# Where an S5 mixer hands over to a gated unit: weight loads, tap shifts and first products in another order

## What is computed

```
def s5_mixer(u, lam_re, lam_im, log_dt, b_re, b_im, c_re, c_im, d_skip, w_glu):
    ...
    bu = jnp.einsum('blgh,gph->blgp', ug, b_bar)
    _, states = lax.associative_scan(_ssm_combine, (a_seq, bu), axis=1)
    y = jnp.einsum('blgp,ghp->blgh', states, c).real.reshape(bsz, length, D_MODEL)
    y = y + d_skip.astype(f32) * u.astype(f32)
    y = jax.nn.gelu(y).astype(u.dtype)
    val, gate = jnp.split(y @ w_glu, 2, axis=-1)
    return val * jax.nn.sigmoid(gate)
...
    for i in range(DEPTH):
        h = rmsnorm(x, norm_mix[i])
        ...
        x = x + mix.astype(x.dtype)
        x = x + swiglu(rmsnorm(x, norm_ffn[i]), ffn_w_gate_up[i], ffn_w_down[i]).astype(x.dtype)
```

## Time and profile before

| | |
|---|---|
| Median of 3 runs | 1955.73 us (1953.88 to 1959.09) |
| Profiled execution, span | 1956.0 us |
| PE busy | 1897.2 us (97%) |
| DVE, ACT, POOL busy | 773.4, 809.7, 849.5 us (40 to 43%) |
| mean granted PE clock | 0.988 of full speed |
| data read from HBM | 165.34 MB |

### The profile page before, as it was taken

How to read it: one execution, slowest core, us unless ns; L and a number is a source line. 1 busy time by engine, 2 the same in 40 slices (tenths; PEclk the granted TensorE clock), 3 DMA queues, 4 the chain that set the end, 5 groups by cost and what they waited for, 6 DMA issues and landing times.

```text
span 1956.0 us, 26523 instructions
## 1 busy us (share of the span) xinstructions
PE 1897.2 (97%) x9610; PEld 1531.5 (78%) x9610; DVE 773.4 (40%) x1386; ACT 809.7 (41%) x1183; POOL 849.5 (43%) x413
## 2 busy tenths in 40 slices
PE   6989999999999999999999999999998999999997
PEld 4878788888887786578888888877885878888886
DVE  7952332222026999815222200455566052222103
ACT  4763344343125434825444421446336154444211
POOL 6544344444434242934344444334334444444441
PEclk9999999999999998999999999999998999999998
DMA  2143232333322132022333333323320323323321
GB/s 106 28 146 98 81 118 86 107 92 101 97 86 88 64 108 65 1 76 87 96 96 97 97 97 97 114 76 108 108 65 1 103 80 97 97 96 97 99 95 43
DMA packets 51833, 170.81 MB, mean 87 GB/s; under 512 B 6696, under 2 KB 11560, under 8 KB 51248
## 3 DMA queue, kind: packets, MB, share of 16 engines
q1 hardware_dynamic: 50320, 164.99, 27.2%
q10 hardware_dynamic: 1440, 4.83, 0.6%
HBM read 165.34 MB, written 2.10 MB: 86 GB/s over the span
## 4 chain that ended last, share of the span: by engine, by line
PE 84%; DVE 10%; DVEq 2%; ACT 1%; issue 1%; DMA 1%; SPq 0%; ACTq 0%
PE ps L238 24%; PE ps L240 24%; PE ps L239 24%; PE ps L1273 2%; PE ps L1287 1%; DVE score L1818 1%; PE ps L1295 1%; PE ps L1550 1%; PE ps L1552 1%; PE ps L1551 1%; DVE h_lo L1196 1%; PE ps L820 1%; DVE top L1814 1%; DVE xT L1119 1%; DMA s_gains<-in_s_gain 1%
## 5 line engine op out<-in xcount | busy, mean ns | idle before, releaser
L228 POOL TENSOR_TENSOR w_lo<-raw,w_hi 128x1024 fp32r<-128x1024 f32 x296 | 713.1, 2417 | 983.5 <-ACT w_hi L221 983.4
L238 PE MATMUL ps<-h_hi,w_hi 128*128 128x512 f32 (+1 forms) x1456 | 570.8, 392 | 4.3 <-DVE h_lo L1196 2.4
L240 PE MATMUL ps<-h_hi,w_lo 128*128 128x512 f32 (+1 forms) x1456 | 567.5, 390 | 0.0
L239 PE MATMUL ps<-h_lo,w_hi 128*128 128x512 f32 (+1 forms) x1456 | 567.3, 390 | 0.0
L221 ACT ACTIVATE w_hi<-raw 128x1024 fp32r<-128x1024 f32 x296 | 311.5, 1057 | 500.4 <-PE ps L240 449.5
L238 PEld LDWEIGHTS ps<-h_hi,w_hi 128*128 128x128 f32 (+1 forms) x1456 | 272.6, 187 | 64.3 <-issue 7.0
L240 PEld LDWEIGHTS ps<-h_hi,w_lo 128*128 128x128 f32 (+1 forms) x1456 | 272.5, 187 | 58.7
L239 PEld LDWEIGHTS ps<-h_lo,w_hi 128*128 128x128 f32 (+1 forms) x1456 | 272.5, 187 | 57.7 <-issue 0.5
L238 PE MATMUL ps<-hid_hi,w_hi 128*128 (+1 forms) x528 | 205.4, 389 | 0.0
L239 PE MATMUL ps<-hid_lo,w_hi 128*128 (+1 forms) x528 | 205.4, 389 | 0.0
L240 PE MATMUL ps<-hid_hi,w_lo 128*128 (+1 forms) x528 | 205.4, 389 | 0.0
(11 more groups left out here) (378 smaller groups left out, 2094.7 us busy)
## 6 DMA issues: line engine op xcount, KB each, us to landing
raw<-in_w_gu SPq DMA_DIRECT2D x132, 512.0 KB, 3.5
raw<-in_w_down SPq DMA_DIRECT2D x66, 512.0 KB, 3.6
raw<-in_w_mix SPq DMA_DIRECT2D x33, 512.0 KB, 3.5
raw<-in_w_dsa SPq DMA_DIRECT2D x29, 512.0 KB, 3.6
raw<-in_w_glu SPq DMA_DIRECT2D x16, 512.0 KB, 3.8
raw<-in_w_out SPq DMA_DIRECT2D x12, 512.0 KB, 3.5
raw<-in_w_o SPq DMA_DIRECT2D x8, 512.0 KB, 3.4
s_x<-in_xs SPq DMA_DIRECT2D x1, 2048.0 KB, 11.4
```

Source lines behind the costliest of these rows:

```text
L228: pool.tensor_tensor(w_lo[slot][:], raw[slot][:], w_hi[slot][:].bitcast(F32), ALU.subtract)\
L238: pe.matmul(o, wh, ah, start=start, stop=False)
L239: pe.matmul(o, wh, al, start=False, stop=False)
L240: return pe.matmul(o, wl, ah, start=False, stop=stop)
```

## The change

Four things move, and nothing is added to what is computed.

1. The first four weight loads are issued by SP ahead of the eight tap shifts of step 7 (`load_first`), and `decay_ready` is no longer waited for.
2. The eight tap shifts of step 7 go on two queues: t = 0, 2, 4, 6 on SP, t = 1, 3, 5, 7 on ACT (`shift`).
3. ACT in step 6 makes the decay table and u_q of step 7 first, issues its four shifts, and only then copies out step 6 (`outputs(6)`). In `finish` two of the three weight splits come ahead of `gelu(6)`.
4. PE multiplies the first three k-tiles of the first pair (18 matmuls) ahead of `turn_outputs(7)`, the rest behind it (`gated_first`, EARLY = 3).

```diff
+        def load_first(sp, view):
+            for u in range(R):
+                sp.dma_start(raw[u][:], view[u]).then_inc(raw_landed[u], 16)
...
-            for u in range(head):
+            for u in range(head if n0 else 0):
                 load(n0 + u, view[u])
...
+        def shift(queue, e, p, tokens):
+            queue.wait_ge(S["conv_ready"], e + 1)
+            queue.wait_ge(S["y_done"], e + 1)
+            for t in tokens:
+                queue.dma_start(toep[p][GH * (CH - 1 - t):P, t, :, :], conv[0:GH * (t + 1), :, :]).then_inc(toep_landed[p], 16)
...
-            s5_steps(sp, shift_taps, shift_taps, shift_taps)
-            sp.wait_ge(S["winT_ready"], NQ)
-            sp.wait_ge(S["wout_ready"], NQ)
-            sp.wait_ge(S["ang_ready"], NQ)
-            sp.wait_ge(S["decay_ready"], NQ)
+                shift(sp, e, p, range(CH))
+            def finish(e, p, use):
+                sp.wait_ge(S["winT_ready"], NQ)
+                sp.wait_ge(S["wout_ready"], NQ)
+                sp.wait_ge(S["ang_ready"], NQ)
+                load_first(sp, d["w_glu"])
+                shift(sp, e, p, range(0, CH, 2))
+            s5_steps(sp, shift_taps, shift_taps, finish)
...
-                angles(e + 1, 1 - p, between=lambda: outputs(e))
-                inputs_out(e + 1, 1 - p)
+                if e < NQ - 2:
+                    angles(e + 1, 1 - p, between=lambda: outputs(e))
+                    inputs_out(e + 1, 1 - p)
+                else:
+                    angles(e + 1, 1 - p)
+                    inputs_out(e + 1, 1 - p)
+                    shift(act, e + 1, 1 - p, range(1, CH, 2))
+                    outputs(e)
             def finish(e, p, use):
+                split_hi(act, 0)
+                split_hi(act, 1)
                 gelu(e - 1, 1 - p)
-                for k in range(LOOK):
-                    split_hi(act, k)
+                split_hi(act, 2)
                 outputs(e)
                 gelu(e, p)
...
             def finish(e, p, use):
                 turn_outputs(e - 1)
                 outputs(e, p, use)
+                next_products()
                 turn_outputs(e)
...
+        def gated_first(pe, ph, kts, free=None):
+            pe.wait_ge(ph.pair_done, ph.before + 1)
+            if free is not None:
+                pe.wait_ge(*free)
+            first = [unit(FIRST[ph.name] + half) for half in range(2)]
+            pe.wait_ge(lo_ready, first[1][1] + 1)
+            for kt in kts:
+                pe.wait_ge(*ph.in_ready(kt + 1))
+                for half in range(2):
+                    last = gated_product(pe, first[half][0], half, kt)
+                    if kt == KT - 1:
+                        last.then_inc(unit_used, 1)
+        EARLY = 3
...
-            gated_tensor(pe, glu)
+            s5_tensor(pe, lambda: gated_first(pe, glu, range(EARLY)))
+            gated_tensor(pe, glu, begun=EARLY)
```

More of the change, by code:

```diff
@@ L752, in s5_vector, with s5_tensor @@
             s5_steps(dve, begin, step, finish)
-        def s5_tensor(pe):
+        def s5_tensor(pe, next_products):
             for n, credits in (("convps", 1), ("w_ready", 2), ("y_done", 2), ("yT_ready", 1)):
@@ L907, in __init__, with gated_product, gated_tensor @@
                 self.name, self.pairs, self.in_ready = name, pairs, in_ready
[L909 to L915, removed]
+        def gated_product(pe, slot, bank, kt):
+            cols = slice(kt * P, (kt + 1) * P)
+            return mm3(pe, ps[:, bank, :], w_hi[slot][:, cols], w_lo[slot][:, cols], h_hi[:, kt, :], h_lo[:, kt, :],
+                       kt == 0, kt == KT - 1)
+        def gated_first(pe, ph, kts, free=None):
[11 more added lines that the diff above has]
+        EARLY = 3
+        def gated_tensor(pe, ph, nm=None, free=None, begun=0):
             def pair(jj, it=None, halves=(0, 1)):
@@ L921, in pair @@
                     for kt in range(KT):
-                        last = products(slot, 2 * jj + half, kt)
+                        last = gated_product(pe, slot, 2 * jj + half, kt)
                     last.then_inc(unit_used, 1)
[L925 to L935, removed]
+            gated_first(pe, ph, range(begun, KT), free)
             if nm is not None:
@@ L2493, in _ @@
             pe.sem_inc(unit_used, 1)
-            s5_tensor(pe)
-            gated_tensor(pe, glu)
+            s5_tensor(pe, lambda: gated_first(pe, glu, range(EARLY)))
+            gated_tensor(pe, glu, begun=EARLY)
             gated_tensor(pe, gu0, norm_f0)
```

## The result

| | before | after |
|---|---|---|
| time, us (median; fastest to slowest) | 1955.56 (1952.96 to 1959.99) | 1962.36 (1958.21 to 1964.67) |
| span of the profiled execution, us | 1956.0 | 1962.5 |
| ratio to before, 95% interval | | 1.0031 (1.0024 to 1.0037) |

The forecast was 1951.4 us with a range up to 1957.8. The changed kernel is 6.8 us slower than before. That is 0.31%, with the interval of the ratio clear of 1. Its span differs by 6.5 us. The tap tables of step 7 did not land at 123.1, but 8 us later, at about 131.4. A span is some 2 us shorter than the time of the same execution (1962.5 of 1964.67 here), so that spans are compared with spans and times with times. The times of after fall in two groups, four at 1958.2 to 1958.8 and sixteen at 1961.7 to 1964.7, so that a median of few executions also depends on how many fell in each.

What follows compares the result with a forecast made beforehand. PE, busy 97%, was taken as the bound, held by tap tables, clock and work ahead of the first weight product. -3.1 (outputs(7)) - 2.4 (early products) + 1.15 (transposes) + 0.1 = -4.3 us: 1951.4 us, range 1948.8 to 1957.8.

Steps and rivals of the forecast that it cites:

- they land at about 123.0: SP's four tap shifts, queued behind the weight loads, land at about 123.0; all taps were taken as there at 123.1.
- the small pieces fit between the loads' turns: On the DMA engines, shift pieces slip in between the weight loads, so the taps are there at 123.1.
- Shifts on two queues: Step 7's eight tap shifts, four on SP and four on ACT: ACT's issues end at 121.0 to 121.7, taps land at 123.1.
- Rival 2: At step 7's taps: xT gets ahead of ACT's last shift, which lands at about 128; 1957.2 or 1958.5 us; chance 0.18.
- last shift should be there 1 us earlier: Argument against Rival 2: ACT's last shift reaches the DMA engines 1 us before xT begins there, at about 123.
- -4.3: Whole handover from step 6 to the first pair: 4.3 us less, first pair ending at 140.5 instead of 144.8; chance 0.55.

Runs made afterwards that it cites:

- e1: The changed kernel with SP issuing the 2 MB load of xT only when the tap tables of step 7 have landed; ratio to before 0.9997.
- e3: The changed kernel with xT loaded by eight DMAs of 256 KB, in 2 KB pieces, same order and queues; ratio to before 1.0004.
- e5: The changed kernel with two weight units ahead of the shifts, the other two and xT issued once the tap tables have landed; 1950.69 us, ratio 0.9971.
- e11: The kernel of e5 without SP's wait for the taps ahead of weight units 2 and 3 and xT; 1954.34 us, ratio 0.9991.
- e7: The kernel of e5 with all eight shifts on SP; ratio to before 0.9988.
- e2: The changed kernel with all eight shifts of step 7 on SP, xT behind them, none on ACT; 1954.19 us, ratio 0.9997.
- e8: The kernel of e5 with the decay table and u_q of step 7 behind ACT's copy of s_y again; ratio to before 0.9997.
- e10: The kernel of e5 once more, on another chip; 1951.27 us, ratio to before 0.9974.

## Why the prediction was wrong, point by point

**Right.** ACT's sequencer runs ahead and issues beside the arithmetic (0.20 us behind the cosine's start; the issues end at 121.71, forecast 121.0 to 121.7, though 0.8 us of offset is in the measured one). The copy of s_y is not late. The decay table comes early: the scan of after starts at 121.76, forecast 120.95 + 0.8, and zout is ready at 125.35, forecast 124.55 + 0.8. The first weight product follows the state products without a gap, and neither POOL nor k-tile 7 is late. The transposes cost their 1.15 us where they now stand.

**The step that failed** is "they land at about 123.0" and "the small pieces fit between the loads' turns", in "Shifts on two queues". On after's times that would be 123.9; PE got its tables at 131.49. Two errors lie in it, and the runs part them:

1. xT. Rival 2 named the mechanism, with a chance of 0.18, against it that "the last shift should be there 1 us earlier". But the comparison was of issue times, and it should have been of when pieces reach a DMA engine. Both queues stood still behind the weight loads until 122, so an issue 1 us earlier or later decided nothing. e1 takes 5.0 us of wait away, e3 4.95 with the same bytes.
2. The four weight loads. Without xT the tables still come for 125.86 (e1; forecast 123.1, or 123.3 with e1's offset of 0.2). The shifts went neither ahead of the units nor beside them: on both queues they took 4.4 to 5.4 us to land in e1, and in after none of ACT's pieces moved from 119 to 122. Then 368 pieces in one microsecond, and some late ones behind them, came on top of the 122.6 that I had for the last unit. Half as many units in front, and the rest held back, brings a landing time of 2.0 us for the last shift (e5). Half as many in front without holding back the rest leaves 4.1 (e11).

**What that cost.** Zout is ready at 125.35 and PE begins at 131.49: 6.1 us. The tap products are no longer hidden behind zout, 1.9 us (131.49 to 133.40). The clock makes state products of 5.1 us (133.40 to 138.51) out of 3.7: 1.4 us. Together 9.4 us on the forecast's -4.3 give +5.1, the measured handover.

**Rival 2's price.** 1957.2 or 1958.5 us, against 1962.36. Its landing at 128 would be 128.8 here and was 131.4: it began xT's turns at 122.6 and gave them 5.2 us, but they went on beyond 128 (23 pieces in the microsecond ahead of it), and the last pieces moved up to 3 us later, with SP's next unit already under way. It also had `outputs(7)` take 6.2 us; it took 7.0. The range ended at this rival's lower price, 1957.2 plus scatter.

**By the Trainium skill**, "DMA: Bandwidth & Descriptors", section "Queues, rings and completion order", a DMA engine serves the queues in turn, a whole packet of many descriptors at a time. The start of after agrees: from 120 to 122, with ACT's first shift issued by 119.78, 192 pieces of 4 KB went ahead, 12 for each DMA engine. So does e11, where nearly the whole last shift then moved in half a microsecond. Beside xT it does not: by that rule ACT's 8 pieces for each engine would have passed in one or two turns, while 26 and 25, then 23 and 23 show turns of one piece each. There the measurement decides; why the turns are so short beside 16 KB pieces is not shown. The other rule that the prediction named, that a second issuing engine saves issue time only, holds against e7: the second queue of e5 saved issue time, worth 2.8 us.

**The chances.** The forecast of -4.3 us had 0.55. It was right for a kernel that holds the shifts' way free (e5, -4.2), and not for the one that was to be judged.

## What to carry to other kernels

Small transfers that an engine will wait for should not share the DMA engines with a transfer of large pieces on another queue. Here an estimate of (pieces on one DMA engine) x (time of one large piece) came within 0.1 us of what 16 KB pieces cost, though the tail behind them was not in it; beside 4 KB pieces only the wait for a first turn was to be seen. Hold the large transfer back until the small ones have landed, put it behind them in one queue (e2), or cut its pieces small (e3). Prefetch only what is needed first ahead of an urgent transfer, here two of four units. When two transfers race, compare when their pieces reach the DMA engines, behind all that is queued there, and not when they are issued.

## What the runs showed of the hardware that I had not expected

- A second queue waits for its first turn behind 4 KB weight pieces: its first packet moved 2.6 us after the end of its issue in after and over 2.3 in e11, where free engines took 0.65 (e5). Beside 16 KB pieces the two queues then take turns piece by piece, 512 B against 16 KB, with 0.62 us for each turn (after, 126 to 128); beside 4 KB pieces they do not (e11, 142 packets against 46 from 124 to 124.5). In 2 KB pieces the same 2 MB delayed the shifts by nothing that can be seen (5.4 us to landing, with and without it).
- The same idle time ahead of a group of matmuls costs clock in one place and not in another. e7 and e8, both with one wait of 2.06 us in this stretch:

```profile
123.00:128.00 5.00, 3.38 (x32) 3.05 (x34) 2.21 (x3) 3.28 (x4) 4.05 (x2) 0.69 0.54 165
```

```profile
123.00:128.00 5.00, 2.74 (x59) 2.46 (x60) 3.35 (x5) 4.97 (x7) 2.80 (x2) 1.00 0.55 191
```

  In e7 (first row, 0.69) PE had idled 0.75 us and done 1.15 us of transposes ahead of that wait; in e8 (second row, 1.00) it had idled 1.67 and then worked 2.2 us, transposes and tap products. Nor does the same history always cost the same: in e1 and e3 it was 0.75 us idle, 1.15 of transposes and 2.7 idle, and the clock from 125 to 126 was 0.61 and 1.00. What makes the difference is open.
- Behind the handover all kernels run the same code, yet from the fifth split to the end the profiled executions took 1807.8 to 1812.3 us: before 1811.5, after 1812.1, e5 1808.6, e8 1812.3, e10 1807.8. So a single span can't settle a question of 2 us here, while the handover, read inside the trace, repeats to 0.1 us (e5 and e10, no wait for the taps in either).
